# Expert results stored row by row, and both fixed experts' token lists ahead of the ranking

## The reference, cut to what matters

```python
def moe_ffn(h, w_router, router_bias, w_gate_l, w_up_l, w_down_l):
    t = h.reshape(b * l, d)
    scores = jax.nn.sigmoid((t @ w_router).astype(jnp.float32))
    sel = scores + router_bias.astype(jnp.float32)
    grp = sel.reshape(-1, N_EXPERT_GROUPS, EXPERTS_PER_GROUP)
    best = jnp.argmax(lax.top_k(grp, TOP_K)[0].sum(axis=-1), axis=-1)
    ...
    _, idx = lax.top_k(masked, TOP_K)
    w = jnp.take_along_axis(scores, idx, axis=-1)
    w = w / w.sum(axis=-1, keepdims=True)
    gates = jnp.sum(jax.nn.one_hot(idx, N_EXPERTS) * w[..., None], axis=1)
    hid = jax.nn.silu(jnp.einsum('nd,edf->enf', t, w_gate_l)) * jnp.einsum('nd,edf->enf', t, w_up_l)
    hid = hid * gates.T[:, :, None].astype(hid.dtype)
    return jnp.einsum('enf,efd->nd', hid, w_down_l).reshape(b, l, d)
```

## Time and profile before

| | |
|---|---|
| median of 3 runs | 814.85 us (814.3 to 821.09) |
| the profiled execution: its own time | 814.5 us |
| its span in the trace | 812.8 us |
| PE busy | 750.6 us, 92% of the span |
| DVE, ACT, POOL busy | 40%, 26%, 17% of the span |
| mixture of layer 0, mixture of layer 1 | from about 262 to 424 us, and from about 643 us to the end |

### The profile page before, as it was taken

One profiled execution on the slowest core, in us unless ns is written; L12 is line 12 of the kernel. 1 busy time (PEld: TensorE's weight loads), 2 busy tenths in 40 slices (PEclk: granted clock), 3 DMA queues, 4 the chain that ended last, 5 costly groups with the idle time before them and its releaser, 6 DMA issues. The chain is left out here.

```text
span 812.8 us, 9495 instructions
## 1 busy us (share of the span) xinstructions
PE 750.6 (92%) x3496; PEld 381.2 (47%) x3496; DVE 328.5 (40%) x865; ACT 212.2 (26%) x484; POOL 141.9 (17%) x238
## 2 busy tenths in 40 slices
PE   3699998999998799999999999888999889999994
PEld 0347553446546444443344755345644644444331
DVE  1302525634735543321282262564643735331236
ACT  1310155824023011101222024592402311101121
POOL 2426041220000200000202403222001110000202
PEclk9799999999999999999999999999999999999998
DMA  8994236899701889999997223354430299999961
GB/s 332 392 354 183 104 110 247 304 361 402 266 1 79 322 327 392 423 423 422 383 350 284 103 104 110 108 182 181 179 104 0 101 411 357 417 423 421 425 245 78
DMA packets 54051, 211.54 MB, mean 260 GB/s; under 512 B 7883, under 2 KB 8755, under 8 KB 41715
## 3 DMA queue, kind: packets, MB, share of 16 engines
q1 hardware_dynamic: 40456, 179.33, 56.3%
q10 hardware_dynamic: 7851, 17.70, 5.9%
q0 software_dynamic: 5696, 13.89, 4.8%
HBM read 202.02 MB, written 13.93 MB: 266 GB/s over the span
## 5 line engine op out<-in xcount | busy, mean ns | idle before, releaser
L2161 PE MATMUL bank<-ring,work 128*64 128x512 f32 (+1 forms) x512 | 158.2, 600 | 3.5 <-DVE work L1537 2.6
L2161 PEld LDWEIGHTS bank<-ring,work 128*64 128x64 f32 (+1 forms) x512 | 59.2, 158 | 96.7 <-issue 93.3
L2177 PE MATMUL bank<-ring,xs_tok 128*64 128x512 f32 (+1 forms) x256 | 79.9, 597 | 3.1 <-DVE xs_tok L1548 2.0
L1548 DVE COPY xs_tok<-bank 128x256 f32<-128x256 f32 x22 | 9.3, 425 | 147.8 <-PE bank L2168 147.7
L1807 PE MATMUL bank<-hT,ring 128*128 128x384 f32 x192 | 62.2, 486 | 0.0
L1703 PE MATMUL bank<-ring,cpad 128*32 128x512 f32 x384 | 48.7, 633 | 10.1 <-DMA ring<-in_w_ada_dram 9.4
L1807 PEld LDWEIGHTS bank<-hT,ring 128*128 128x128 f32 x192 | 36.5, 190 | 25.0
L2177 PEld LDWEIGHTS bank<-ring,xs_tok 128*64 128x64 f32 (+1 forms) x256 | 28.1, 157 | 40.5 <-issue 37.1
L1775 PE MATMUL bank<-ring,hT 128*128 128x512 f32 x96 | 43.9, 614 | 2.3 <-ACT hT L799 2.3
L978 ACT ACTIVATE xs_tok<-bank 128x256 f32<-128x256 f32 x22 | 8.5, 386 | 143.3 <-PE bank L2161 143.3
L2056 PE MATMUL bank<-ring,xn 128*128 128x512 f32 x96 | 43.5, 596 | 0.0
(11 more groups left out here) (383 smaller groups left out, 1075.1 us busy)
## 6 DMA issues: line engine op xcount, KB each, us to landing
ring<-in_w_ada_dram SPq DMA_DIRECT2D x48, 1024.0 KB, 8.5
ring<-in_w_gate_dram SPq DMA_DIRECT2D x32, 1024.0 KB, 12.7
ring<-in_w_up_dram SPq DMA_DIRECT2D x32, 1024.0 KB, 16.3
ring<-in_w_down_dram SPq DMA_DIRECT2D x32, 1024.0 KB, 14.3
ring<-in_w_in_dram SPq DMA_DIRECT2D x16, 1024.0 KB, 14.9
ring<-in_w_out_dram SPq DMA_DIRECT2D x8, 1024.0 KB, 10.3
y_exp<-qkv ACTq DMA_DIRECT2D x16, 512.0 KB, 8.3
xpad<-gate_rows ACTq DMA_DIRECT2D x6, 512.0 KB, 5.2
```

Source lines behind the costliest of these rows:

```text
L1548: dve.tensor_copy(hidT[:, b, :], bank[2][:, 0:F]).then_inc(s_htc, 1)
L2161: last = mm(bank[b][i * n:(i + 1) * n, :].rearrange("p (i f) -> p i f", i=2), rows_T[:, kt * P + i * n:kt * P + (i + 1) * n], gate_up_of(s ...
L2177: last = mm(bank[5 + hf][i * n:(i + 1) * n, :], hidT[:, b, f * P + i * n:f * P + (i + 1) * n], w[:, f, hf * 512:(hf + 1) * 512], start=f = ...
```

## The change

Four things change.

- The selections of both fixed experts are made one after the other, and the list of block 1 is made two steps into the ranking, not behind it. On PE the lists of blocks 0 and 1 follow each other, and the idle-time products (5 and 4 of them) become 10 behind both.
- The selections of blocks 5 and 6 come behind DVE's copy of block 0's rows, those of 2 to 4 stay ahead of it.
- The stores of blocks 0 to 7 move from ACT (one plain DMA of 512 KB) to POOL: an indirect DMA with a row number per place (`y_at`). Places that hold no token get a number beyond the bound, so their rows aren't written. POOL issues the first four stores between the gathers of blocks 6 to 10 and the last four behind them. DVE makes `y_at` from `idx` by two operations.
- Since some rows of `y_exp` are now never written, SP fills it once, in layer 0, with 8 copies of a 512 KB input from DRAM to DRAM, ahead of its wait for the order; POOL waits for them before the first store.

```diff
+                        if l == 0 and len(experts) == 1:
+                            for e in range(STORED):
+                                sp.dma_start(y_exp[e * CAP:(e + 1) * CAP, :], x_prompt[0]).then_inc(s_filled, 16)
                         sp.wait_ge(s_order, l + 1)
...
+                def rows_stored(e):
+                    if e == 0:
+                        pool.wait_ge(s_yat, l + 1)
+                        pool.wait_ge(s_filled, 16 * STORED)
+                    pool.wait_ge(s_yc, 2 * e + (2 * NB * l + 4))
+                    pool.indirect_dma_start(
+                        out=y_exp[:, :], out_offset=bass.IndirectOffsetOnAxis(ap=y_at[:, e:e + 1], axis=0),
+                        in_=y_buf(e), in_offset=None,
+                        bounds_check=STORED * CAP - 1, oob_is_err=False).then_inc(y_stored[e % 2], 16)
+
                 for b in range(NB):
+                    if b > AHEAD:
+                        rows_stored(b - AHEAD - 1)
                     pool.wait_ge(s_idx, len(LISTS) * l + list_of(b) + 1)
...
+                for e in range(NB - AHEAD - 1, STORED):
+                    rows_stored(e)
...
                     for hf in range(2):
                         act.activation(y_buf(e)[:, hf * 512:(hf + 1) * 512], bank[5 + hf][:, :],
                                        ACT.Copy).then_inc(s_yc, 1)
-                    if e >= STORED:
-                        return
-                    act.wait_ge(s_yc, 2 * e + (2 * NB * l + 4))
-                    dma(y_exp[e * CAP:(e + 1) * CAP, :], y_buf(e)).then_inc(y_stored[b], 16)
...
                 fixed_one_hot(0)
+                fixed_one_hot(1)
                 dve.tensor_copy(count, bank[7][:, 96:96 + E])
...
-                slot_tokens(0)
...
                 step(dve.tensor_tensor(perm_tmp, rep(key, RANKED), bc(key, RANKED), ALU.is_ge))
+                slot_tokens(0)
                 step(dve.tensor_reduce(rank.unsqueeze(2), perm_tmp, AX.X, ALU.add))
+                slot_tokens(1)
...
-                fixed_one_hot(1)
-                slot_tokens(1)
...
-                one_hots(*LISTS[2])
+                one_hots(LISTS[2][0], ROWS_AT)
...
                 copy_rows(0, 0)
+                one_hots(ROWS_AT, LISTS[2][1])
                 slot_tokens(2)
...
+                step(dve.tensor_scalar(y_past[:, :], idx[:, 0:STORED], NT * P - 0.5, float(STORED * CAP), ALU.is_gt, ALU.mult))
+                dve.tensor_tensor(y_at[:, :], y_past[:, :], y_row[:, :], ALU.add).then_inc(s_yat, 1)
...
                 lists(0)
-                clock_kept(2, 5)
                 lists(1)
-                clock_kept(2, 4)
+                clock_kept(2, 10)
```

More of the change, by code:

```diff
@@ L208, in hybrid_step @@
         e_row = sb("e_row", E)
+        y_row, y_past = sb("y_row", STORED), sb("y_past", STORED)
         idx = ctx.enter_context(nc.sbuf_tensor("idx", [P, E], u32))
+        y_at = ctx.enter_context(nc.sbuf_tensor("y_at", [P, STORED], u32))
         y_idx = ctx.enter_context(nc.sbuf_tensor("y_idx", [P, 2, NT], u32))
@@ L333, in hybrid_step @@
             "slot_tokens_made", "result_rows_made"))
+        s_yat, s_filled = sem("store_rows_made"), sem("store_rows_filled")
         s_bt, s_btc, s_h = sem("h_transposed_back"), sem("h_rows_copied"), sem("h_rows_stored")
@@ L403, in hybrid_step @@
         LISTS = ((0, 1), (1, 2), (2, 7), (7, NB))
+        ROWS_AT, AHEAD = 5, 6
         list_of = lambda e: next(i for i, (a, b) in enumerate(LISTS) if a <= e < b)
@@ L570, in _ @@
             pool.iota(iota[:, CAP + 6:CAP + 6 + E], pattern=[[CAP, E]], base=-1, channel_multiplier=0)
+            pool.iota(iota[:, 208:208 + STORED], pattern=[[CAP, STORED]], base=0, channel_multiplier=1)
             at = {r: b * CAP + HALF * i for b, (p, part) in enumerate(BLOCKS) if RANK_AT[p]
@@ L739, in _ @@
                 for b in range(2):
-                    pool.wait_ge(y_stored[b], 16 * stores_of(b) * (l + 1) + 16)
+                    pool.wait_ge(y_stored[b], 16 * stores_of(b) * (l + 1))
                 for t in range(NT):
@@ L751, in _ @@
             act.sem_inc(s_yc, 2)
-            for b in range(2):
-                act.sem_inc(y_stored[b], 16)
             for dst, src in (
@@ L982, in store @@
                     act.wait_ge(s_dn, e + (NB * l + 1))
-                    act.wait_ge(y_stored[b], 16 * (min(e // 2, stores_of(b)) + stores_of(b) * l + 1))
+                    if e >= 2 or l:
+                        act.wait_ge(y_stored[b], 16 * (min(e // 2, stores_of(b)) + stores_of(b) * l))
                     for hf in range(2):
@@ L1053, in _ @@
             dve.tensor_copy(e_row[:, :], iota[:, CAP + 6:CAP + 6 + E])
+            dve.tensor_copy(y_row[:, :], iota[:, 208:208 + STORED])
             dve.wait_ge(s_const, 1)
@@ L1556, in _ @@
                 slot_tokens(3)
+                dve.wait_ge(s_idx, len(LISTS) * (l + 1))
+                step(dve.tensor_scalar(y_past[:, :], idx[:, 0:STORED], NT * P - 0.5, float(STORED * CAP), ALU.is_gt, ALU.mult))
+                dve.tensor_tensor(y_at[:, :], y_past[:, :], y_row[:, :], ALU.add).then_inc(s_yat, 1)
                 for e in range(NB):
```

## The result

The changed kernel is **slower by 0.4%**: 818.74 us (815.86 to 823.36, 20 runs) against 816.33 us of the kernel before in the same set (810.8 to 821.63, 20 runs), ratio 1.0044, 95% interval 1.0028 to 1.006. The prediction was 807.4. Between the mixtures both traces have short stretches of low clock at other places than the trace before. They come and go from one execution to the next, so I compare stretches that begin and end at the same two steps and not times from the start.

What follows compares the result with a forecast made beforehand. TensorE, busy 92% of the span, was taken as the bound, with time to win at each layer's first two blocks and last one. 4.5 + 1.5 - 0.3 + 1.8 = 7.5 us, from 814.5 to 807.0, stated as 807.4; bounds 805 to 815.

Steps and rivals of the forecast that it cites:

- The fill: Layer 0, ahead of the order: 4.2 MB written while DMA engines are partly idle, cost taken as 0, bounds 0 and 3 us.
- rival (d): The fill isn't hidden, its large pieces hold the gate vectors for 10 us and more: 3 us lost, 810; chance 0.05.
- The head of layer 0: First two blocks: earlier gather 1 ends TensorE's wait, 2.8 us, and full clock adds 1.7; gain 4.5 us, bounds 1.1 and 4.5.
- The 1.7 us of clock: Layer 0's head: 16 products at full clock take 7.11 us in place of 8.81; bounds 0 and 1.7.
- The head of layer 1: First two blocks: earlier block 0 products and no wait for gather 1; gain 1.5 us, bounds 1.0 and 1.6.
- the heads' gain reaches the end: Both layers: the heads' 4.5 and 1.5 us were counted in full in the gain of the whole time.
- The stores: Stores by rows from POOL: last store takes 8.5 us, bounds 7.9 and 16.8, and lands about 1.3 us later.
- 3.2 us of traffic less: Full stretch ahead of the tail: six stores leave out 1.35 MB of tokenless rows, 3.2 us at 0.42 MB/us.
- the 1.8 us of layer 1's tail: End of layer 1: weight waits go, last gather lands earlier; gain 1.8 us, bounds a gain of 2.5, a loss of 1.3.
- Layer 0's tail: End of layer 0: results' gathers start 1.3 us later; loss 0.3 us, bounds a gain of 1.0, a loss of 1.6.
- Rival (b): Last store takes 16.8 us and lands 9.6 us later in each layer: slower, 825; chance 0.07.
- The range: Whole kernel: all bounds of the terms together were said to give 805 to 815 us.

Runs made afterwards that it cites:

- e1: The changed kernel, but SyncE waits for the loads of both gate vectors before it issues the 8 fill stores; ratio 1.0032 to the kernel before.
- e2: The kernel before plus the 8 fill stores at the changed kernel's place, store 0 waiting for them; old lists, plain stores; ratio 1.0052.
- e4: The kernel before with stores by rows on GpSimd and the fill issued only after both gate vectors are loaded; old lists; ratio 1.003.
- e13: The kernel of e1, but every place of a stored block gets its own row as address, so no row is dropped; ratio 1.0 to the kernel before.
- e9: The changed kernel with 8 more stores of the fill's size into a buffer nothing reads, 8.4 MB in place of 4.2; ratio 1.0212 to the kernel before.
- e14: The kernel of e1, but a layer's eight stores are plain ones of 128 whole rows, issued by GpSimd; ratio 0.9994 to the kernel before.

## Why the prediction was wrong, step by step

- **The fill: the term that was off by most.** It said "I take 0", with bounds 0 and 3, for VectorE's 8.61 us of slack. It costs 4.9 to 5.2 us in three traces, 3.1 and 4.2 us between timed kernels of one set (1.0 between the changed kernel and e1, of two sets). The load of the gate vectors was named as what it could hit, and the rival (d) had the mechanism, but with the wrong engine and 0.05: ahead of the load ScalarE waits for six small stores to land, and behind the load, in the same queue, stands the copy for TensorE, with no slack. The trace of before showed ScalarE's load and copy 7 us apart. What it didn't show is that the last state store would need 29.9 us in place of 19.1.
- **The head of layer 0: mechanism right, sizes partly.** Gather 1 took 6.7 us here (6.5 taken), 6.7 to 9.4 in the thirteen kernels with the new lists. The 1.7 us of clock were no gain of the change: e2 and e4 have the old lists, waits of 2.27 and 1.65 us for gather 1, and 16 products in 7.11. The 8.81 of the earlier trace rows was one execution's.
- **The head of layer 1**: 0.7 us in this trace where 1.5 were forecast, since gather 1 took 9.3 us (8.2 to 9.6 in the others, and 8.4 was the edge).
- **That the heads' gain reaches the end: failed, and it is the step that matters.** Slack was worked out for pair 1's weights only, "more than 5 us"; the last pair's waits of 0.70 and 1.08 were named at the tail, but taken as gone with 3.2 us less traffic. In the trace of before the last up weights of layer 0 landed at 390.5 and were used at 390.67; in layer 1 TensorE waited 0.70 for them. A gain at the head had 0.2 us and less than nothing to go. Forecast were 6.0 us from both heads; the lists alone gave none of it (0.7 and 0.5 us slower, within noise), and the waits for the last up weights grew from 0 and 0.70 to 1.02 and 2.98.
- **The stores.** The last one took 8.4 us in e4's chain of waits and 8.6 in e1's, as forecast (8.5); 590 rows a layer are right, "3.2 us of traffic less" is wrong in its effect, 0 (e13). With it fell the 1.8 us of layer 1's tail: from block 1's first products to the last down product it took 2.9 us more than before (130.4 against 127.5), of which 1.7 are slow products behind the wait. Layer 0's tail, forecast at a loss of 0.3, lost 1.0 (127.9 against 128.6 less 1.70).
- **Rival (b)** didn't come: GpSimd never waited longer than 9.3 us for a last store. The kernel was slower by (d) at more than its 3 us in the traces, with no gain to set against it.
- **The range.** "All bounds together give 805 to 815" leaves out the fill's own bound of 3 us: 1.1 + 1.0 - 1.6 - 1.3 - 3.0 is a loss of 3.8 us, so the upper end was 818.7. The measured 818.74 lies there. That is no hit: the fill cost more than its bound, and the rest came about by a wait that the sum didn't have.

The Trainium skill bears on two of these points. "DMA: Bandwidth & Descriptors" (section Queues, rings and completion order) says that each DMA engine takes turns between the queues at packet level, which the prediction weighed for the gathers. ScalarE's queue beside the fill agrees with it: 181 packets against 180 in 8 us, the ones of 256 bytes, the others up to 32 KB. The gathers aren't described by it: 3.6 to 4.6 us well ahead of the loads, 8.7 to 9.9 behind the first. The same section says that the write which raises a semaphore lands only after every earlier write of that DMA engine, across its queues. No run here shows that this cost anything: in e9 ScalarE's stores were signalled at 228.9 and 234.6, before the fill's last landing at 237.9.

The sum by what was measured: fill +5.0 by the traces (3.1 and 4.2 by the timed pairs), lists +0.6, stores 0 by e13 and e14 (up to 2.4 by e4): 3.7 to 5.6 us against 3.6 (2.3 to 4.9).

No version tried that computes the whole result beats the kernel before. e14 and e13, without the price of the early fill, equal it.

## What to carry to other kernels

Before a gain at the head of a stage is counted, look at the last transfer that the stage waits for: if it lands within a microsecond of its use, the stage has two limits, and only what starts the stream earlier or makes it shorter gains. A "free" bulk write in large packets is paid by whoever waits for a store made of many small packets in another queue beside it, and by everything in that engine's queue behind this wait. (Whether state stores in larger pieces would take the price away was not tried.) One slow group of products in one execution is not a gain to be had; look at a second execution first.

## What the hardware showed that I had not expected

- A gather of 128 rows of 4 KB takes 3.6 to 4.6 us when the first weight load comes 1.9 us behind it or later, 8.7 to 9.9 when started 0.9 to 1.2 us behind the first, and still 6.7 to 9.6 when started 0.4 to 0.7 us ahead of it.
- Rows dropped by an address beyond the bound are still packets, and in full traffic they save bytes (18.72 against 22.28 MB) and no time.
- Four stores of 64 KB, in packets of 256 bytes, landed 29.9 us after the issue of the last beside 4.2 MB of another queue's copies in packets of 32 KB, and 19.1 us without these; the two queues moved 181 and 180 packets in the same 8 us. Two stores of 12 KB behind them landed after 18 us in place of 7, and after 29 us beside 8.4 MB.
- After waits of TensorE of 2.0 to 4.7 us the next 32 products took 8.59 to 10.06 us in ten cases and 7.09 in five (after 2.04, 2.05, 2.13, 2.45 and 3.11); after waits below 2.0 always 7.09. Over the 8.78 of layer 1 in the changed kernel (777.2 to 786.0 us) the granted clock was 0.81, a mix of the two levels, in the stretch before it 1.00. The length of the wait alone doesn't decide.
